# First norm of a two-stream transformer step: conditioning weights in row chunks on two queues, squares summed per token

## The reference

```python
def adaln(cond, w_ada, b_ada):
    m = jax.nn.silu(cond) @ w_ada + b_ada          # w_ada: 1024 x 9216
    return m.reshape(cond.shape[:-1] + (1, N_MOD, D_MODEL))
def rmsnorm(x, gain):
    y = xf * lax.rsqrt(jnp.mean(xf * xf, axis=-1, keepdims=True) + EPS)
    return (y * gain.astype(jnp.float32)).astype(x.dtype)
def modulated_norm(x, gain, shift, scale):
    return rmsnorm(x, gain) * (1 + scale) + shift
x = x + 0.5 * mod[..., 2, :] * swiglu(modulated_norm(x, norm_ffn1, mod[..., 0, :], mod[..., 1, :]), ...)
```

## Time and profile before

| | us |
|---|---|
| three runs, lowest, median, highest | 1584.05, 1586.75, 1586.85 |
| profiled execution, its own time | 1581.51 |
| span of the profiled execution | 1579.7 |
| VectorE busy | 1062.2 (67%) |
| ScalarE busy | 591.4 (37%) |
| mean granted TensorE clock | 0.991 of full speed |

### The profile page before, as it was taken

How to read it: one execution, slowest core, us unless ns; L and a number is a source line. 1 busy time by engine, 2 the same in 40 slices (tenths; PEclk the granted TensorE clock), 3 DMA queues, 4 the chain that set the end, 5 groups by cost and what they waited for, 6 DMA issues and landing times.

```text
span 1579.7 us, 26562 instructions
## 1 busy us (share of the span) xinstructions
PE 1523.3 (96%) x10204; PEld 1435.9 (91%) x10204; DVE 1062.2 (67%) x1908; ACT 591.4 (37%) x1138; POOL 196.2 (12%) x158
## 2 busy tenths in 40 slices
PE   6899999999999999998998999999999999999998
PEld 4899999999999999987887988999999999998886
DVE  5978777787374767554867887678887777763334
ACT  4522222221122533533653214264554444444323
POOL 0000000000000000020006677566000000000000
PEclk9999999999999999999997999999999999999999
DMA  9354454544244312211001101002213322222222
GB/s 303 118 158 142 140 158 148 156 143 157 83 138 147 94 54 67 68 46 49 28 28 34 41 15 28 21 28 83 65 41 94 94 80 80 80 80 67 72 75 94
DMA packets 186937, 141.96 MB, mean 90 GB/s; under 512 B 8544, under 2 KB 169829, under 8 KB 186725
## 3 DMA queue, kind: packets, MB, share of 16 engines
q1 hardware_dynamic: 164149, 118.26, 24.4%
q10 hardware_dynamic: 22704, 22.55, 4.5%
HBM read 137.34 MB, written 3.45 MB: 89 GB/s over the span
## 4 chain that ended last, share of the span: by engine, by line
PE 86%; DVE 7%; SPq 2%; ACT 2%; issue 1%; POOL 1%; DMA 1%; DVEq 0%; ACTq 0%
PE ps L2234 14%; PE ps L2236 14%; PE ps L2235 14%; PE ps L2396 5%; PE ps L2398 5%; PE ps L2397 5%; PE ps L2468 3%; PE ps L2467 3%; PE ps L2466 3%; PE ps L2898 3%; PE ps L2902 3%; SPq L525 2%; PE ps L2669 1%; PE ps L2905 1%; PE ps L2690 1%
## 5 line engine op out<-in xcount | busy, mean ns | idle before, releaser
L2234 PE MATMUL ps<-h_hi,w_lo 128*128 128x320 f32 x1152 | 364.0, 316 | 9.3 <-DVE h_lo L1377 4.0
L2236 PE MATMUL ps<-h_hi,w_hi 128*128 128x320 f32 x1152 | 356.4, 309 | 0.0
L2235 PE MATMUL ps<-h_lo,w_hi 128*128 128x320 f32 x1152 | 356.4, 309 | 0.0
L1330 DVE TENSOR_TENSOR w_lo<-w_raw,w_hi 128x1024 fp32r<-128x1024 f32 x120 | 147.6, 1233 | 232.0 <-ACT w_hi L718 231.7
L2234 PEld LDWEIGHTS ps<-h_hi,w_lo 128*128 128x128 f32 x1152 | 216.9, 188 | 15.9 <-DVE h_lo L1377 6.9
L2235 PEld LDWEIGHTS ps<-h_lo,w_hi 128*128 128x128 f32 x1152 | 217.1, 188 | 0.8 <-issue 0.2
L2236 PEld LDWEIGHTS ps<-h_hi,w_hi 128*128 128x128 f32 x1152 | 216.7, 188 | 0.0
L718 ACT CAST w_hi<-w_raw 128x1024 fp32r<-128x1024 f32 x120 | 125.6, 1048 | 207.1 <-PE ps L2236 109.5
L1464 DVE SCALAR_TENSOR_TENSOR ada_acc<-ada_ffn,cond,ada_acc 128x256 f32<-128x256 f32 x392 | 161.8, 478 | 1.2
L2234 PE MATMUL ps<-act_hi,w_lo 128*128 128x320 f32 (+1 forms) x352 | 108.9, 309 | 2.1 <-DVE mods L1493 2.1
L2236 PE MATMUL ps<-act_hi,w_hi 128*128 128x320 f32 (+1 forms) x352 | 108.5, 308 | 0.0
(11 more groups left out here) (384 smaller groups left out, 3200.4 us busy)
## 6 DMA issues: line engine op xcount, KB each, us to landing
w_raw<-in_w_ffn_in SPq DMA_DIRECT2D x64, 512.0 KB, 3.8
w_raw<-in_w_ffn_out SPq DMA_DIRECT2D x44, 512.0 KB, 3.7
ada_ffn<-in_w_ada ACTq DMA_DIRECT2D x43, 512.0 KB, 3.5
w_raw<-in_w_in SPq DMA_DIRECT2D x28, 512.0 KB, 3.7
ada_ffn<-in_w_ffn_in SPq DMA_DIRECT2D x20, 512.0 KB, 3.7
ada_ffn<-in_w_ada SPq DMA_DIRECT2D x13, 512.0 KB, 4.5
ada_tile<-in_w_ada SPq DMA_DIRECT2D x10, 512.0 KB, 7.8
w_raw<-in_w_out SPq DMA_DIRECT2D x8, 512.0 KB, 3.4
```

What stands on the lines that cost most here:

```text
L1330: nc.vector.tensor_tensor(w_lo[at], w_raw[s][:], w_hi[at].bitcast(F32), ALU.subtract)\
L2234: nc.tensor.matmul(out, lo, xh, start=start, stop=False)
L2235: nc.tensor.matmul(out, hi, xl, start=False, stop=False)
L2236: return nc.tensor.matmul(out, hi, xh, start=False, stop=stop)
```

## The change

The first 2048 columns of w_ada come as eight row chunks of 128 rows x 2048 columns (`ada_k`, 1 MB each, one contiguous 8 KB piece in a partition). ScalarE issues chunks 0, 1, 2, then x, then chunk 3, ahead of all else; SP issues chunks 4 to 7 behind the small loads, with fold and weight tile 0 behind chunk 4 and weight tile 1 behind chunk 5. TensorE takes the first nine blocks of 128 columns of every chunk (matmuls of 512, 512 and 128 columns, accumulating over the chunks), VectorE the other seven (two operations of 896 elements on every chunk, one for each of the two conditionings), with w_low(0) and w_low(1) behind chunks 4 and 5. VectorE's accumulator is reduced over groups of 32 rows by one transposing reduce and finished by one matmul with fold. The squares are taken over x_tok, in place, one instruction for each of the five groups of 128 tokens, with ScalarE's accumulator giving the sum per token; Ln and Exp run on 128 x 5 values, and six matmuls spread the roots over the partitions. The eight additions of squares, the two mean matmuls and the 24 column-sum matmul records are gone. The table load for Ln and Exp moves ahead of the copies of x.

```diff
-ADA_PE, ADA_DVE = 10, 3
-SQ_BASE, PART_BASE = [0, 8, 12, 16], [None, 0, 4]
+ADA_PE, ADA_WIDE = 9, 7
+HEAD_SUMS = 2
+HEAD_BANKS = [2, 3, 7, 0, 1]
+HEAD_SPREAD = [(0, 0, 0, 0, P), (0, 1, P, 0, P), (0, 2, 2 * P, 0, HT - 2 * P),
+               (1, 2, 0, HT - 2 * P, P), (1, 3, 3 * P - HT, 0, P), (1, 4, 4 * P - HT, 0, P)]
+SQ_BASE, PART_BASE = [0, 0, 4, 8], [None, 0, 4]
...
+        def head_load(eng, k):
+            eng.dma_start(ada_k[k][:], w_ada[0, k * P:(k + 1) * P, 0:2 * KD * P]).then_inc(ada_landed[k], 16)
...
         def _(sp):
...
+            for k in range(4, KD):
+                head_load(sp, k)
+                if k == 4:
+                    sp.dma_start(fold[:], consts[:, N_SMALL:N_SMALL + P]).then_inc(fold_in, 16)
+                if k in (4, 5):
+                    ffn_load(k - 4)
+            for i in range(2, 4):
+                ffn_load(i)
+
             sp.wait_ge(x_copied, 2 * NT)
-            sp.wait_ge(ada_summed, ADA_DVE + 1)
+            sp.wait_ge(ada_summed, HEAD_SUMS)
...
         def _(act):
...
+            for k in range(3):
+                head_load(act, k)
+            act.dma_start(x_tok[:, 0, :], x_prompt[0]).then_inc(x_in, 16)
+            act.dma_start(x_tok[:, 1:NT, :], x_sample[0].rearrange("(t p) d -> p t d", p=P)).then_inc(x_in, 16)
+            head_load(act, 3)
             act.wait_ge(cols_turned, 2)
...
+            load_power_table()
             for i in range(2 * NT):
                 t, q = i // 2, i % 2
                 act.wait_ge(x_turned, i + 1)
-                nc.scalar.copy(x_t[:, 4 * q:4 * q + 4, t * P:(t + 1) * P], heads4(ps[:, 2 + i % 4, :], P)).then_inc(x_copied, 1)
+                nc.scalar.copy(x_t[:, 4 * q:4 * q + 4, t * P:(t + 1) * P], heads4(ps[:, HEAD_BANKS[i % len(HEAD_BANKS)], :], P)).then_inc(x_copied, 1)
-            act.wait_ge(x_copied, 2 * NT)
-            load_power_table()
-            for k in range(KD):
-                square_of(k, 0, None)
-            root(0, 0)
-            root(0, 1)
+            act.wait_ge(x_turned, 2 * NT)
+            for t in range(NT):
+                ins = nc.scalar.activation(x_tok[:, t, :], x_tok[:, t, :], ACT.Square, accum_out=tok_rs[:, t:t + 1])
+            ins.then_inc(sq_tok, 1)
+            act.wait_ge(sq_tok, 1)
+            act.wait_ge(ones_set, 1)
+            rs = tok_rs[:, 0:NT]
+            nc.scalar.activation(rs, rs, ACT.Ln, bias=eps_col[:], scale=1.0 / D).then_inc(log_ready, 1)
+            act.wait_ge(log_ready, 1)
+            nc.scalar.activation(rs, rs, ACT.Exp, scale=-0.5).then_inc(log_ready, 1)
             w_high(0, 0)
+            for half in range(2):
+                act.wait_ge(mean_mm, half + 1)
+                nc.scalar.copy(half_of(rstd, half), ps[:, half, 0:HT]).then_inc(rstd_ready, 1)
             w_high(1, 1)
-            act.wait_ge(ada_used, ADA_PE)
             for n in range(0, ADA_PE, 4):
                 end = min(n + 4, ADA_PE)
+                act.wait_ge(ada_used, n // 4 + 1)
                 ins = nc.scalar.copy(ada_row[:, n * P:end * P], ps[0:2, 4 + n // 4, 0:(end - n) * P])
...
         def _(dve):
...
+            def ada_chunk(k):
+                dve.wait_ge(ada_landed[k], 16)
+                for g in range(2):
+                    w, a, col = ada_k[k][:, ADA_PE * P:2 * KD * P], ada_wide_acc[:, g * wide:(g + 1) * wide], cond[:, k, g:g + 1]
+                    if k == 0:
+                        ins = nc.vector.tensor_scalar(a, w, col, None, ALU.mult)
+                    else:
+                        own.wait_back(1)
+                        ins = nc.vector.scalar_tensor_tensor(a, w, col, a, op0=ALU.mult, op1=ALU.add)
+                    own.mark(ins)
...
-            ada_setup(0)
             for k in range(KD):
-                add_square(k, 0)
-            ada_setup(1)
-            ada_setup(2)
-            w_low(0, 0)
-            w_low(1, 1)
+                ada_chunk(k)
+                if k in (4, 5):
+                    w_low(k - 4, k - 4)
+            own.wait_back(0)
+            nc.vector.tensor_reduce(head_sums[:], ada_wide_acc[:].rearrange("p (n r) -> p n r", r=32), AX.X, ALU.add,
+                                    apply_transpose=True).then_inc(ada_wide_read, 1)
...
+            own.mark(nc.vector.tensor_tensor(mods[:, 0:ADA_PE, :], ps[:, 7, 0:2 * ADA_PE].rearrange("p (m a) -> p m a", a=2),
+                                             spread(cols_a[:, 0:ADA_PE], 2), ALU.add))
+            dve.wait_ge(ada_summed, HEAD_SUMS)
+            for q in range(4):
+                rows = slice(32 * q, 32 * q + 32)
+                sums = ps[rows, 3, 0:8 * ADA_WIDE].rearrange("p (g u q) -> p u g q", g=2, q=4)[:, :, :, q]
+                own.mark(nc.vector.tensor_tensor(mods[rows, ADA_PE:2 * KD, :], sums, spread(cols_a[rows, ADA_PE:2 * KD], 2), ALU.add))
...
         def _(pe):
...
+            def ada(a):
+
+                pe.wait_ge(ada_landed[a], 16)
+                for i, n in enumerate((512, 512, ADA_PE * P - 1024)):
+                    ins = nc.tensor.matmul(ps[0:2, 4 + i, 0:n], cond[:, a, :], ada_k[a][:, i * 512:i * 512 + n],
+                                           start=(a == 0), stop=(a == KD - 1))
...
+            pe.wait_ge(cond_ready, 2)
+            for a in range(3):
+                ada(a)
             pe.wait_ge(x_in, 32)
             for i in range(2 * NT):
                 t, q = i // 2, i % 2
-                if i >= 4:
-                    pe.wait_ge(x_copied, i - 3)
+                if i in (7, 9):
+                    ada(3 if i == 7 else 4)
+                if i >= len(HEAD_BANKS):
+                    pe.wait_ge(x_copied, i - len(HEAD_BANKS) + 1)
...
                 ins.then_inc(x_turned, 1)
...
+            ada(5)
+            ada(6)
+            pe.wait_ge(log_ready, 2)
+            for half, t, at, a, b in HEAD_SPREAD:
+                ins = nc.tensor.matmul(ps[:, half, at:at + b - a], tok_rs[:, t:t + 1].broadcast_to([P, P]), ident[:, a:b],
+                                       start=True, stop=True)
+                if at + b - a == HT:
+                    ins.then_inc(mean_mm, 1)
+            ada(7)
             pe.wait_ge(ada_rows, 1)
...
+            pe.wait_ge(fold_in, 16)
+            pe.wait_ge(ada_wide_read, 1)
+            nc.tensor.matmul(ps[:, 3, 0:8 * ADA_WIDE], fold[:], head_sums[:], start=True, stop=True).then_inc(ada_summed, 1)
             first_ffn()
```

More of the change, by code:

```diff
@@ L325, in hybrid_step @@
             holder(s)("act_space", [P, 2 * NJ * T])
-            ada_wide_acc = [holder(s)(f"ada_wide_acc{i}", [P, 2 * PAIR]) for i in range(ADA_DVE)]
+            ada_wide_acc = holder(s)("ada_wide_acc", [P, 2 * ADA_WIDE * P])
         with ExitStack() as s:
@@ L515, in _ @@
             sp.dma_start(rows_b[61:62, :], diff_norm).then_inc(small_in, 16)
[L516 to L526, removed]
             def w_load(n, s, src, first=False):
@@ L738, in root @@
             def root(nth, half):
-                bank = half if nth == 0 else 4 + half
                 act.wait_ge(mean_mm, 2 * nth + half + 1)
-                nc.scalar.activation(half_of(rstd, half), ps[:, bank, 0:HT], ACT.Ln, bias=eps_col[:]).then_inc(log_ready, 1)
+                nc.scalar.activation(half_of(rstd, half), ps[:, 4 + half, 0:HT], ACT.Ln, bias=eps_col[:]).then_inc(log_ready, 1)
                 act.wait_ge(log_ready, 2 * nth + half + 1)
@@ L1761, in _ @@
             dve.wait_ge(cond_ready, 2)
-            ada_setup(0)
             for k in range(KD):
-                add_square(k, 0)
-            ada_setup(1)
-            ada_setup(2)
-            w_low(0, 0)
-            w_low(1, 1)
-            dve.wait_ge(cols_ready, 2)
-            dve.wait_ge(ada_summed, ADA_DVE + 1)
-            own.link(nc.vector.tensor_tensor(mods[:, 0:2 * KD, :], ps[:, 7, 0:4 * KD].rearrange("p (m a) -> p m a", a=2),
-                                             spread(cols_a[:, 0:2 * KD], 2), ALU.add))
+                ada_chunk(k)
@@ L2247, in mean @@
             def mean(nth, half):
-                if nth == 0:
-                    pe.wait_ge(sq_added, SQ_BASE[1])
-                else:
-                    pe.wait_ge(added_half[half], PART_BASE[nth] + len(PARTS[nth]))
-                bank = half if nth == 0 else 4 + half
-                nc.tensor.matmul(ps[:, bank, 0:HT], ones_d[:], half_of(sumsq, half), start=True, stop=True).then_inc(mean_mm, 1)
+                pe.wait_ge(added_half[half], PART_BASE[nth] + len(PARTS[nth]))
+                nc.tensor.matmul(ps[:, 4 + half, 0:HT], ones_d[:], half_of(sumsq, half), start=True, stop=True).then_inc(mean_mm, 1)
             def by_parts(nth, slots, ready, whole):
@@ L2275, in by_parts @@
                             mean(nth, 1)
-            def ada(n):
-                pe.wait_ge(ada_landed[n], 16)
-                for a in range(KD):
-                    ins = nc.tensor.matmul(ps[0:2, 4 + n // 4, (n % 4) * P:(n % 4 + 1) * P], cond[:, a, :],
```

(13 more changed lines are left out.)

34 lines of the change are left out of this document (11 added, 23 removed).

## The result

| us | before | after |
|---|---|---|
| median of the runs taken together (19 and 19) | 1585.46 | 1587.77 |
| lowest, highest | 1581.37, 1588.37 | 1586.85, 1592.12 |
| profiled execution, its span | 1581.51, 1579.7 | 1592.12, 1590.3 |
| first matmul of the first feed-forward | 48.14 | 53.00 |

What follows compares the result with a forecast made beforehand. The stage before the first feed-forward matmul was taken as bound by one SP DMA queue. T 21.2 + 32.4 put that matmul at 53.6 against 48.14, 5.5 us later; on the median 1586.75 that gave 1592.2 us, range 1586 to 1600.

Steps and rivals of the forecast that it cites:

- T: Start of the x transposes on TensorE, forecast at 21.2 us, with 17.3 and 27.2 as lower and upper ends.
- the last copy: End of the last x copy: ten transpose groups, two conditioning chunks between them and the copy, at T + 10.0.
- the squares: ScalarE's five squares of 1024 with an accumulator, at 1.24 us each: 6.2 us, ending at T + 16.2.
- Ln to cast: ScalarE's Ln, Exp and their gaps, 0.6 us, then w_high(0), 1.04 us, ending at T + 17.85.
- the cast to the head: From w_high(0)'s end to the first feed-forward matmul: VectorE's remaining work, fold matmul, mods sums and what follows, 14.5 us.
- The cause: VectorE's w_low(0), between chunks 4 and 5, waits for ScalarE's w_high(0), holding up later chunks; over 8 us idle.
- turns of packets: The two DMA queues alternate packet by packet, so T = 21.2; the likeliest case, chance 0.52.
- three chunks on TensorE then end at 21.2: With cond delayed to 15.1, TensorE's three chunks end at the same instant as T, costing nothing more.
- the longer pause: TensorE's longer pause before the first feed-forward matmul, with its clock at 0.50, allowed 0 to 0.5 us.
- rival 4: 8 KB packets run no faster than 347 GB/s, T grows by 1.4 us; chance inside the others' widths.
- Rival 3: ScalarE's chain is not last, only DMA and VectorE remain: first matmul 41.3, 6.9 us earlier, 1579.9 us; chance 0.08.
- The rest at nothing: Other edits, such as the table load, weight tile issues and first ada_ffn loads, were priced at no time.

Runs made afterwards that it cites:

- the 4 KB one: The changed kernel with every row chunk loaded as two DMAs of 1024 columns, so 4 KB packets instead of 8 KB: 1585.95 us, one run.
- the x-first kernel: The changed kernel with x issued first on ScalarE's queue and its transposes first on TensorE: 1578.87 us, ratio 0.9965 to the kernel before.
- the ordered one: The kernel with chunks alternating between queues, changed to all eight behind x on ScalarE's queue, chunks 0 and 1 between x transposes: 1579.08 us, ratio 0.9969.
- the last three kernels: All with x first: weight tiles behind chunk 7, 1581.91 us; chunks alternating between the queues, 1578.75 us; all chunks on ScalarE's queue, 1579.08 us.

## Why the prediction was right

Slower was forecast (5.5 us) and slower it was (3.8, interval 2.5 to 5.1; 4.86 in the head). The 1592.2 itself is 4.4 above the median after. 0.6 of that is the head (53.6 forecast, 53.00 found) and 1.3 the median of the three runs that I started from, 1586.75 where the larger number of runs has 1585.46. The other 2.5 are the difference between the head, 4.86 us, and the medians, 2.3 us. I put it down to the half-clock stretches that come and go behind the head (the lowest runs, 1581.37 and 1586.85, are 5.5 us apart); that is not shown. The 53.6 is also closer than its terms: by T +0.5, the last copy -0.4, the squares -1.0, Ln to cast -0.1 and the cast to the head +0.5 the errors nearly cancel.

- **The cause**: right. The wait for w_high(0) was named with its place and its length (over 8 us; 10.2), and moving w_low away took it off the way of the chunks (1.1 and 1.3 us of waiting for the casts are left behind the reduce). That the new cover is the whole of VectorE's remaining work was right too: 38.01 to 48.82 is 10.8 us, 10.85 worked out.
- **T**: 21.70 for 21.2, and partly by luck. The landing of x was by turns of packets (20.7 for 21.2). The term that set T was the other, "three chunks on TensorE then end at 21.2": cond came 0.65 earlier (14.45), and the chunks took 7.27 us where nine blocks of 0.225 each gave 6.1. The other shape hardly matters (2.10 us for a chunk from 25 us on, 2.03 by the 0.225); it is the clock, of which I had not thought here. Had it been full, T would have been 20.7; in four other kernels with three chunks ahead of x it was 22.3 to 23.7, and 21.4 in the 4 KB one.
- **T to the last copy**: 10.0 worked out, 9.56 found.
- **The squares**: the mis-sized term. 6.2 us worked out, 5.3 found (31.17 to 36.47, one every 1.04). In the earlier trace rows the read of the accumulator follows the square and a gap follows it; in a row of squares the next one starts within the read. I had added a pause that exists only at the end.
- **The cast to the head**: from the end of w_hi (37.98) 15.0 us for the 14.5 of the text: the fold matmul and its handovers took 0.83 instead of 0.5 (0.65 for the matmul, at a granted clock of 0.50 behind 6.9 us of idle TensorE; 0.40 in the x-first kernel). This lies inside the 0 to 0.5 us that I had given the longer pause.
- **The reduce**: 2.04 worked out from the slope of the plain reduce, 2.04 found.
- **8 KB packets** at 421 to 428 GB/s: above the 408 I priced them at; rival 4 was wrong. The last chunk landed at 33.1 for 33.4.
- **The small loads**: 11.66 for 12.3. The forecast is close, but nearly half of the delay is not the turns it was put down to, if the rest goes with the packet size, as the 4 KB kernel suggests.
- **Rival 3** named 12.6 as the T from which ScalarE's chain is no longer last, and 41.3 as the head then. The x-first kernel has T 11.4 and 42.96. That fits the threshold; the price was 1.7 low, since chunk 7 came at 34.7 (33.4 in the rival), and the rest is the tail from the reduce on.
- **The rest at nothing**: the first SiLU of the feed-forward was as late as the first matmul (4.87, 4.86), so neither the weight tiles nor the ada_ffn loads gave or took anything, nor did the half clock behind the first matmul, which ends near 58 (5 us behind it) where it ended at 51 (3 us) before.

The Trainium skill, "DMA: Bandwidth & Descriptors", "Queues, rings and completion order", has each DMA engine go round its queues a packet at a time. The landings of x in three kernels (the one after, all chunks on ScalarE's queue, 4 KB packets) and of the chunks in the ordered one agree to 0.5 us with turns of single row pieces; that of x in the x-first kernel missed its forecast by 2.0, as told there. The Trainium skill's "Issuing engines are not separate DMA queues", on the same page, lets a second issuing engine save issue time only. The runs agree on the rate, but the order and the split of the same transfers over the queues decided which of them came first: chunk 3 landed at 28.9, 18.4 and 20.9 in the last three kernels, and the reduce started at 39.63, 36.16 and 34.00.

## What to carry to other kernels

A faster transfer is worth what the first consumer can take: before splitting a load over two queues, write down per consumer what it needs first, and put the start of the longest chain (here x, not the weights) at the head of a queue. An in-order engine turns one early dependent instruction into a stall of all that stands behind it; move it behind the work that has its data, but not onto the end of the chain if it fits in a wait on the way. Two queues loaded with equal packets deliver at half speed each, and a small transfer in small packets holds up its own queue by as many turns, so split by what may be late, not by count.

## What had not been expected of the hardware

- Small loads beside a second queue are late by more than the turns of packets account for: twelve loads, done at 5.9 us with the queue to themselves, at 10.1 to 10.9 beside 4 KB packets and 11.7 to 12.1 beside 8 KB ones.
- fold, 64 KB in 512 B packets, took from 15.4 to 18.0 us beside 8 KB packets of the other queue (2.6 us, where 1.05 MB take 2.5 at 427 GB/s), and so put the chunks out of order.
- fp32 matmuls of 512 columns at the start of the kernel took 1.05 us against 0.59 later, under a recorded clock of 1.00.
- ScalarE's square of 1024 with accumulator repeats every 1.04 us: the read of 0.19 to 0.29 costs nothing while another square follows.
